# Reordered start and indexer turn in a one-core hybrid token-mixer kernel: full weight units first, x in eighths, idle transposes, half-block indexer queries

## The reference, cut to what matters

```
h    = rmsnorm(x) * pre_norm_g
proj = h @ w_in                    # 2048 x 18776, cut into columns for all branches
y_a  = diff_attention(q, k, v) * silu(z)            # 8 heads
y_b  = mlstm(silu(conv(qk)), v, gates, o) * silu(z) # 4 heads
c    = rmsnorm(dsa_kv);  ik = rmsnorm(idx_k)
isc  = sum_h relu(iq_h . ik) * iw_h                 # 16 indexer heads of 64, top 64 keys kept
y_c  = latent_attention(dsa_q, c, top64(isc)) * silu(z)
mixed = sum_b sigmoid(gate_b) * (y_b @ w_branch_b)
out  = x + rmsnorm(mixed @ w_out) * post_norm_g
```

## Time and profile before

| | us |
|---|---|
| median of 3 runs | 1127.31 |
| lowest, highest | 1126.73, 1128.7 |
| the profiled execution's own time | 1126.54 |
| its span, first to last instruction | 1124.7 |

### The profile page before, as it was taken

One profiled execution on the slowest core, in us unless ns is written; L12 is line 12 of the kernel. 1 busy time (PEld: TensorE's weight loads), 2 busy tenths in 40 slices (PEclk: granted clock), 3 DMA queues, 4 the chain that ended last, 5 costly groups with the idle time before them and its releaser, 6 DMA issues.

```text
span 1124.7 us, 15512 instructions
## 1 busy us (share of the span) xinstructions
PE 1103.7 (98%) x5191; PEld 916.1 (81%) x5191; DVE 660.6 (59%) x927; ACT 541.0 (48%) x720; POOL 64.1 (6%) x111
## 2 busy tenths in 40 slices
PE   7999999999999999999899999999999999999997
PEld 7788888888887888889787778888888888888886
DVE  5744444665666676767767566665456555556545
ACT  6644444555554554545345544454544544445442
POOL 1000000100100011121210000000000000000000
PEclk9999999999999999999899999999999999999999
DMA  9666666656555556666566557555555566667553
GB/s 249 222 190 192 197 189 191 182 170 174 171 176 170 168 150 176 189 177 206 150 175 182 172 148 220 189 169 140 188 162 163 149 197 194 190 205 279 186 188 113
DMA packets 112406, 205.19 MB, mean 182 GB/s; under 512 B 11064, under 2 KB 15728, under 8 KB 111984
## 3 DMA queue, kind: packets, MB, share of 16 engines
q1 hardware_dynamic: 112368, 204.70, 60.5%
HBM read 202.57 MB, written 2.10 MB: 182 GB/s over the span
## 4 chain that ended last, share of the span: by engine, by line
PE 93%; DVE 3%; DMA 1%; ACT 1%; issue 1%; SPq 0%; DVEq 0%; ACTq 0%
PE stream L1253 29%; PE stream L1255 28%; PE stream L1254 28%; DVE wlo L814 1%; PE stream L1385 1%; PE mixer L1527 1%; DMA raw<-in_w_in 1%; DMA mixed<-in_x 0%; DVE xboth L834 0%; PE stream L1386 0%; ACT whi L548 0%; PE mixer L1554 0%; PE mixer L1543 0%; PE mixer L1351 0%; PE mixer L1326 0%
## 5 line engine op out<-in xcount | busy, mean ns | idle before, releaser
L814 DVE TENSOR_TENSOR wlo<-raw,whi 128x1024 fp32r<-128x1024 f32 (+1 forms) x378 | 460.8, 1222 | 425.6 <-ACT whi L548 423.7
L548 ACT ACTIVATE whi<-raw 128x1024 fp32r<-128x1024 f32 (+1 forms) x378 | 397.7, 1054 | 559.0 <-PE stream L1255 521.6
L1253 PE MATMUL stream<-whi,xboth 128*128 128x512 f32 (+1 forms) x1248 | 493.9, 396 | 6.7 <-DVE area L979 4.0
L1255 PE MATMUL stream<-whi,xboth 128*128 128x512 f32 (+1 forms) x1248 | 485.9, 389 | 0.0
L1254 PE MATMUL stream<-wlo,xboth 128*128 128x512 f32 (+1 forms) x1248 | 485.0, 389 | 0.0
L1253 PEld LDWEIGHTS stream<-whi,xboth 128*128 128x128 f32 x1248 | 235.3, 189 | 58.4 <-issue 6.1
L1255 PEld LDWEIGHTS stream<-whi,xboth 128*128 128x128 f32 x1248 | 235.1, 188 | 49.2
L1254 PEld LDWEIGHTS stream<-wlo,xboth 128*128 128x128 f32 x1248 | 235.6, 189 | 45.8
L1253 PE MATMUL stream<-whi,yhi 128*128 128x512 f32 x192 | 76.7, 399 | 0.0
L1255 PE MATMUL stream<-whi,ylo 128*128 128x512 f32 x192 | 74.9, 390 | 0.0
L1254 PE MATMUL stream<-wlo,yhi 128*128 128x512 f32 x192 | 74.8, 389 | 0.0
(11 more groups left out here) (249 smaller groups left out, 592.0 us busy)
## 6 DMA issues: line engine op xcount, KB each, us to landing
raw<-in_w_in SPq DMA_DIRECT2D x288, 512.0 KB, 3.8
raw<-in_w_branch SPq DMA_DIRECT2D x48, 512.0 KB, 4.5
raw<-in_w_out SPq DMA_DIRECT2D x32, 512.0 KB, 4.2
mixed<-in_x SPq DMA_DIRECT2D x4, 512.0 KB, 5.7
raw<-in_w_in SPq DMA_DIRECT2D x8, 256.0 KB, 4.0
area<-in_x SPq DMA_DIRECT2D x2, 1024.0 KB, 8.9
out<-area SPq DMA_DIRECT2D x8, 256.0 KB, 2.3
raw<-in_dsa_w_uv SPq DMA_DIRECT2D x4, 256.0 KB, 2.9
```

The costliest lines, as they stand in the source:

```text
L548: nc.scalar.activation(whi[:, slot, :, 0:width], raw[:, slot, :, 0:width], ACT.Copy).then_inc(whi_ready, 1)
L814: nc.vector.tensor_tensor(wlo[:, slot, :, 0:width], raw[:, slot, :, 0:width], whi[:, slot, :, 0:width].bitcast(F32), ALU.subtract).then_in ...
L1253: nc.tensor.matmul(to, left_hi[:, kt, tokens], high, start=first, stop=False)
L1255: last = nc.tensor.matmul(to, left_lo[:, kt, tokens], high, start=False, stop=final)
```

## The change

It does four things.

1. **Order of the start.** The first two groups of the differential attention (`PA0`, full 512-column units) now run first, then the narrow `PS`, then `PA1` (two groups), then `PA` with two turns. x is loaded in eighths (256 columns), each ahead of the unit that needs it. PE no longer turns all of x first: it turns eighth 0, multiplies unit 0, turns eighths 1 and 2, multiplies unit 1, turns 3, and so on.
2. **Unit 0 in two k-tiles**, with its own semaphores, so that its first half can be loaded, rounded, split and multiplied by itself.
3. **`keep_busy`**: 7 transposes of the identity before eighth 0 is turned and 9 after it, into a bank that nothing reads.
4. **The indexer's turn**: in the first and the last two units of each group blocks 0 and 1 of both units run before blocks 2 and 3 of both (`project_iq_pair`); `take_iq` stands one unit earlier; in turn 2 the mLSTM gate arithmetic moves from unit 12 to unit 14, behind `take_iq`.

The normalisations that DVE and ACT did in one piece behind `PS` are hung into the units of `PA1` (units 0, 1, 3 and 4). The convolution's rows are turned at the end of `PA` and not at the start.

```diff
-X_LOADS = 4
+X_LOADS = 8
-PS = Part(0, 0, 1, FULL_UNITS, 1)
-PA = PS.next(4, 2 * FULL_UNITS, 2)
+PA0 = Part(0, 0, 1, 2 * FULL_UNITS, 2)
+PS = PA0.next(1, FULL_UNITS, 1)
+PA1 = PS.next(1, 2 * FULL_UNITS, 2)
+PA = PA1.next(2, 2 * FULL_UNITS, 2)
...
+            sp.dma_start(rows_g[:, :], pre_norm_g[0].rearrange("(b d) -> b d", d=P)).then_inc(g_landed, 16)
+            for u in range(FULL_UNITS):
+                load_x(u)
+                load_first(u)
...
# ScalarE
             for b in range(8):
                 act.wait_ge(x_turned, b + 1)
                 for k in range(2 * b, 2 * b + 2):
                     nc.scalar.activation(xhi[:, k, :], x_banks[b][...], ACT.Copy, ...).then_inc(xhi_ready, 1)
+                if b == 0:
+                    for j in range(UNIT_KT):
+                        act.wait_ge(raw_landed[0] if j else half_landed, 16)
+                        nc.scalar.activation(whi[:, 0, j, :], raw[:, 0, j, :], ACT.Copy
+                                             ).then_inc(whi_ready if j else half_whi, 1)
+                else:
+                    round_unit(PA0, 0, b - AHEAD)
...
# VectorE
-                    if take and v % FULL_UNITS == FULL_UNITS - 2:
+                    if take and v % FULL_UNITS == FULL_UNITS - 3:
                         take_iq(v // FULL_UNITS)
...
-                    if v == 12:
+                    if v == (14 if take else 12):
...
# TensorE
-            for b in range(8):
-                turn_x(b)
-
-            pe.wait_ge(xlo_ready, 4)
+            def keep_busy(n):
+                for _ in range(n):
+                    nc.tensor.transpose(stream[0][1][:, 0:P], ident[:, :], ident[:, :])
+
+            keep_busy(7)
+            turn_x(0)
+            keep_busy(9)
             for u in range(FULL_UNITS):
+                if u == 1:
+                    for b in range(1, 3):
+                        turn_x(b)
                 pe.wait_ge(xlo_ready, UNIT_KT * (u + 1))
-                multiply(PS, 0, u, u, FULL_UNITS, 0, xhi, xlo, SMALL)
+                multiply(PA0, 0, u, u, FULL_UNITS, 0, xhi, xlo)
+                if 0 < u < FULL_UNITS - 2:
+                    turn_x(u + 2)
...
+            def project_iq_pair(v):
+                for blocks in ((0, 1), (2, 3)):
+                    for n in (v, v + 1):
+                        project_iq(n, blocks)
...
                     if i is IQ_TURN:
-                        project_iq(v)
+                        if u in (0, FULL_UNITS - 2):
+                            project_iq_pair(v)
+                        elif u not in (1, FULL_UNITS - 1):
+                            project_iq(v, range(4))
```

More of the change, by code:

```diff
@@ L68 @@
 KV0, IK0, IW0, IF0, SMALL = 0, 256, 320, 336, 344
-X_LOADS = 4
+X_LOADS = 8
+X_COLS = D_MODEL // X_LOADS
 GROUP = 512
@@ L584, in _ @@
[L584 to L592, removed]
+            act.wait_ge(rstdx_ready, 2)
@@ new lines, in _ @@
+            take_da(PA0, 0, 0, 0)
+            for u in range(FULL_UNITS, 2 * FULL_UNITS):
+                round_unit(PA0, 0, u)
+            take_da(PA0, 0, 1, 0)
+            for u in range(FULL_UNITS):
+                round_unit(PS, 0, u)
+            take_group(PS, 0, FULL_UNITS, PS.group0 % 2, [small[:, t, :] for t in range(TILES)], SMALL)
+            for g in range(2):
+                for u in range(FULL_UNITS):
+                    round_unit(PA1, 0, g * FULL_UNITS + u)
+                    if g == 0 and u == 1:
+                        act.wait_ge(lam_sum_ready, 2)
+                        nc.scalar.activation(lam2, lam2, ACT.Exp).then_inc(lam_exp_ready, 1)
+                        act.wait_ge(row_ready, 1)
+                        nc.scalar.activation(forget_t, forget_t, ACT.Exp).then_inc(row_act, 1)
+                    if g == 0 and u == 2:
+                        act.wait_ge(row_act, 1)
+                        nc.scalar.activation(forget_t, forget_t, ACT.Ln, bias=one).then_inc(row_act, 1)
+                    if g == 0 and u == 3:
+                        act.wait_ge(kv_ms_ready, 1)
+                        nc.scalar.activation(rstdkv[:, 0:4], rstdkv[:, 0:4], ACT.Sqrt).then_inc(kv_std_ready, 1)
+                take_da(PA1, 0, g, 1)
@@ L811, in split_unit @@
                 slot = (part.unit0 + n) % RING
-                width = SMALL if part is PS and n < FULL_UNITS else GROUP
+                width = unit_width(part, n)
                 dve.wait_ge(whi_ready, part.unit(i, n) + 1)
@@ L847, in _ @@
             nc.vector.tensor_scalar(half_rstdx, rstdx, 0.5, None, ALU.mult).then_inc(rstdx_ready, 1)
-            for u in range(FULL_UNITS // 2, FULL_UNITS):
+            for u in range(FULL_UNITS, 2 * FULL_UNITS):
+                split_unit(PA0, 0, u)
+            for u in range(FULL_UNITS):
                 split_unit(PS, 0, u)
-            dve.wait_ge(consts_landed, 6 * 16)
-            dve.wait_ge(banks_free, 4 + 2 * PA.group0)
-            for t in range(TILES):
-                last = nc.vector.tensor_tensor(gate_in[:, t, :], small[:, t, IF0:IF0 + 2 * ML_HEADS], gate_b[:, :],
-                                               ALU.add)
@@ L857, in _ @@
-            steps.step(last)
-            steps.step(nc.vector.tensor_scalar(forget_t, gate_in[:, :, ML_HEADS:], -1.0, None, ALU.mult))
-            nc.vector.tensor_tensor(forget_t, gate_in[:, :, ML_HEADS:], forget_t, ALU.min).then_inc(row_ready, 1)
-            steps.step(nc.vector.tensor_tensor(lam_in[:, 0:4:2, :], lam_in[:, 0:4:2, :], lam_in[:, 1:4:2, :],
-                                               ALU.mult))
-            for n in range(2):
-                nc.vector.tensor_reduce(lam2[:, n:n + 1], lam_in[:, 2 * n, :], AX.X, ALU.add).then_inc(lam_sum_ready, 1)
@@ L1244, in multiply @@
                 slot = (part.unit0 + k) % RING
-                pe.wait_ge(wlo_ready, part.unit(i, k) + 1)
+                halves = part is PA0 and k == 0
+                if not halves:
+                    pe.wait_ge(wlo_ready, part.unit(i, k) + 1)
                 for j in range(UNIT_KT):
+                    if halves:
+                        pe.wait_ge(wlo_ready if j else half_wlo, 1)
                     kt = UNIT_KT * u + j
@@ L1372, in project_iq @@
                 pe.wait_ge(wlo_ready, PC.unit(IQ_TURN, v) + 1)
-                for j in range(4):
+                for j in blocks:
                     if u == 0:
```

201 lines of the change are left out of this document (124 added, 77 removed).

## The result

The changed kernel takes **1118.32 us** (median of 4 executions, 1117.65 to 1119.46) against 1127.83 (4 executions) of the kernel before beside it on the same chip: ratio 0.9917, 95% interval 0.99 to 0.9934. The profiled execution took 1117.77 us, its span 1116.0, against 1126.54 and 1124.7 before.

A forecast was written before the change was run, and what follows sets the result against it. TensorE was busy 1103.7 of 1124.7 us, leaving only idling, half clock and the start. Start +2.95, convolution rows +0.1, indexer's entry 0 and exit -6.4 gave -3.3 to -3.4: forecast 1123.5 us, 8-in-10 range 1119.5 to 1127.2.

The forecast's parts named there:

- Entry net 0: Going into the indexer's turn: 1.0 to 1.1 us saved, then lost to a 1.2 us wait ahead of the scores.
- Exit -6.4: Between turns 2 and 3: the wait of 4.1 us goes, and with it 2.3 us of low clock.
- Rival C: Indexer's turn: its wait only moves, bringing low clock (+2.3) or keeping half the 4.1; 1125.7 to 1127 us, chance 0.11.
- the low clock in half of unit 0: Start: six matmuls of unit 0 at 0.43 us and six at 0.227, so unit 0 takes 3.9 us.
- the low clock behind the wait ahead of unit 1: Start: about 3.1 us of idling before unit 1 brings the clock down, costing 1.5 us (bounds 0 and 2.3).
- rival A: Start: clock high at 8.7 and through the wait ahead of unit 1; 1120.8 or 1119.5 us, chance 0.2.
- first product: Start: first full-width matmul at 8.7 us, 5.6 earlier than before, with the norm weights landed at 3.4.
- chain to unit 1: Start: `xhi`, rounding and split for unit 1 run in series behind the transposes of eighths 1 and 2, 3.96 us.
- later waits on `wlo`: Units 3, 5 and 7: chains of later eighths end after TensorE is ready, 1.5 us, less low-clock cover: 1.3.
- all other work up to there: Unit 1 to end of `PA`: old work without unit 0, 187.2 us, plus 2.2 for transposes of eighths 3 to 7.
- Rival B: Start: idle transposes do nothing for the clock, unit 0 takes 5.1 us; +2.7 at the start, 1126.2 us, chance 0.13.
- Rival D: First group: repeated waits for the chain `xhi`, `whi`, `wlo` keep the clock low throughout; slower, 1137 us, chance 0.06.

The follow-up runs named there:

- pairs only: The change with `project_iq` in pairs, but `take_iq` and the gates where they stood before on VectorE: 1125.24 us, ratio 0.9983 to the kernel before.
- no pairs: The change with `project_iq` unit by unit instead of in pairs, `take_iq` and the gates still moved: 1120.71 us, ratio 0.9942 to the kernel before.
- `ml_cT` first: The change with the first `take_iq` put behind the step that makes `ml_cT`, which the scores wait for: 1117.89 us, ratio 0.9912 to the kernel before.
- the change run again: The change itself, unaltered, on another chip: 1118.96 us against 1126.44 for the kernel before, ratio 0.9929.
- the start alone: The change with the indexer's pairs, earlier `take_iq` and moved gates undone: 1125.59 us, ratio 0.9994 to the kernel before.
- seven idle transposes: The change with the first 7 idle transposes kept and the 9 behind eighth 0 left out: 1119.49 us, ratio 0.9937 to the kernel before.
- no idle transposes: The change with all 16 idle transposes taken out: 1119.49 us, ratio 0.9939 to the kernel before.
- The indexer's part alone: The kernel before with only the pairs, `take_iq` one unit earlier and the gates behind unit 14: 1121.28 us, ratio 0.9958 to the kernel before.
- turning eighth 1 early: The change with eighth 1 turned ahead of unit 0, 5 idle transposes in place of 9: 1116.07 us, ratio 0.9906 to the kernel before.

## Why the prediction was wrong

The forecast sum was -3.3 against the profiled execution; the trace shows -8.8 (1126.54 to 1117.77). The 5.5 between them are 3.9 in the start and 1.6 behind the row turns.

**The indexer's turn was right, in each term.** Entry net 0: the gain is 2.53 ahead of it (499.38 to 496.85, where the turn began) and 2.45 behind it, with a new wait of 1.26 against 1.2 forecast. Exit -6.4: measured 6.36. The cause held too: the kernels without the pairs and with the pairs only show that the moves on DVE's queue remove the 4.0, and the low clock behind it goes with it. The pairs were forecast to gain 1.0, which `take_iq` ahead of `ml_cT` takes back. They gain 1.2 (no pairs), and putting `ml_cT` first gives 1.54 back. Rival C did not come: a wait of 1.26 ahead of the scores was not followed by the low clock.

**The step that failed is the clock in the start**: two terms of the sum, the low clock in half of unit 0 (forecast 1.2, measured 0) and the low clock behind the wait ahead of unit 1 (forecast 1.5, measured 0). I wrote that unit 0 runs half at the low clock, since in the kernel before the clock rose "about 8 us after TensorE's first work", and that the wait ahead of unit 1 costs 1.5 more. That took the 8 us of before as a delay of its own, although its transposes stood apart with gaps of some 0.7 us; I named these gaps only against rival A. Here TensorE worked nearly without a gap from 2.56 on, and the clock rose 4 us later. That the missing gaps did it is not shown: in the change run again TensorE worked as closely from 2.70 on, and its pace fell to 0.23 only at 12.17, 9.5 us later. What is shown is that the delay is no constant.

| term, end of `PA` | forecast | measured |
|---|---|---|
| first product | 8.7 | 8.08 |
| unit 0 | 3.95 | 2.81 |
| chain to unit 1 | 3.96 | 3.82 |
| low clock behind the wait | 1.5 | 0 |
| later waits on `wlo` | 1.3 | 1.2 |
| all other work up to there | 189.4 | 188.95 |
| end of `PA` | 208.8 | 204.86 |

The differences are 0.6, 1.1, 0.1, 1.5, 0.1 and 0.45, together the 3.9. The later waits are read from starts: from unit 1 (14.71) to unit 7 (34.71) there are 20.0 us. Unit 1 takes 2.83 and each of the five eighths turned there takes 3.20 with its unit, 18.8 in all, which leaves 1.2: 0.27 and 0.28 ahead of units 3 and 5 and 0.64 ahead of unit 7, where I forecast 0.35, 0.35 and 0.8. The table of waits has only 0.5 of it (3.3 less 2.79). Only the two clock terms are a wrong mechanism. The first product came sooner because the norm weights, issued alone, were there at 2.56 and not at 3.4; of that 0.84, about 0.2 went into a longer chain behind them. The chain in series was sized well. The last 0.45 is a size of the old work that I took from profiled waits, and stays open.

For the start rival A came in the profiled execution, at chance 0.2; the median of 1118.32 is still below A's 1119.5. Yet it is not a rule that the clock is high: among the seven profiles with both groups of idle transposes and the change's order in the start, the first product found it high in six; the change run again had nine matmuls low, at +1.98. And of the eight profiles with that wait of 2.8 us and the clock high ahead of it (the change, the change again, the start alone, `ml_cT` first, no pairs, pairs only, seven idle transposes, no idle transposes) three showed it low behind: `ml_cT` first, no idle transposes, and pairs only, there after five more matmuls at the high clock. So my two terms are prices that fall due in one of seven and three of eight; with the 1.98 and 1.31 that they cost when they did, I estimate 0.3 and 0.5 us in the mean, where I had put 1.2 and 1.5. The wait of 4.0 us was followed by the low clock in all three profiles that have it.

**Rival B is refuted**, and with it, for this kernel, the sentence of the Trainium skill, page "TensorE: Matmul & The Clock Gate", section "Part 4: PE-mode transpose", that the high clock state does not engage for transposes: 421 to 273 ns among idle transposes and nothing else. Without them unit 0 ran at 0.43 throughout, which is what B priced. **Rival D** did not come; at most 18 matmuls ran low, in the kernel without idle transposes.

**What the sum didn't ask at all** is whether the profiled execution of before was a typical one. It held a fall of the clock behind the row turns, 1.6 us, that no edit touches, and the execution of the change didn't. A difference of two profiles is good to about that much. The medians spread around the profiles' 8.8: the change gained 9.5 us in the first comparison and 7.5 in the second (1126.44 to 1118.96). The indexer's part alone gained 5.3 (1126.58 to 1121.28) and the start alone 1.0, with an interval that reaches no gain.

**Open.** That these two don't add up to 9.5 is not settled. Falls of the clock that come in some executions and not in others cost 1.3 to 2 us each, which is of the right size, but a time without a profile doesn't show its clock. Nor does any run here show what decides in one execution between the two courses of the clock: with `ml_cT` first and in the change run again the nine idle transposes took the same 2.13 us, all at the low clock, and the first product was at high clock in the one (8.09) and low in the other (8.19).

## What to carry to other kernels

Price the chains of latency and the order of the queues: these terms came out within about 0.2 us, and the best further gains (2.3 to 2.9 us in the median for turning eighth 1 early, 1.54 in the trace for `ml_cT` first) came from asking which instruction the next engine waits for and putting it first. Give the clock a chance, not a price: the same program had its first product at either clock, so weigh what a low stretch costs by how often profiles show it, and check a profiled execution for low granted clocks away from the change before you take a sum against it. Idle work ahead of the first product went with an earlier high clock in six of seven profiles but with no clear gain in the median (0.5 to 1.2 us); behind the first product it brought nothing.

## What the runs showed of the hardware

- Transposes alone took TensorE to its high clock: 421 to 273 ns a piece, at about 6.6 us in the change, before any product.
- The same program showed both courses: first product at 8.08 with a pace of 0.23, and at 8.19 with nine matmuls at 0.43. The granted clock prints as 1.00 there in both (from 2 us on), so in the start the pace has to be read.
- Eight small matmuls of 4 rows (1.92 us) were followed by the low clock in 3 of 14 profiles, at a cost of 1.5 to 1.7 us.
- Behind idle time at the high clock: 1.2 us, never low; 2.8 us, low in 3 of 8; 4.0 us, low in 3 of 3.
- A load of 8 KB that was the first of the program landed 1.6 us after its issue, where the fastest of the weight pieces took 2.6.
